# Normalisation and first projections in one stage: two weight chunks projected group by group of tokens

## The chip, the cores and the metric

One core of a Trainium2 chip runs the whole layer in one launch. The time is the device time of one execution in microseconds (us), three executions of the kernel before, and their median. One execution more was recorded by the profiler; all rows below are from it. TensorE is PE in the rows (PEld its weight loads), VectorE is DVE, ScalarE is ACT, GpSimd is POOL, SyncE is SP. SP and ACT each issue transfers (SPq, ACTq).

## What is computed

A layer of a streaming encoder: 2048 tokens of width 1024, float32. What matters here is its beginning:

```
c_act = silu(c)
mod = c_act @ ada_w[l] + ada_b[l]
sh1, sc1, g1, sh2, sc2, g2 = jnp.split(mod, 6, axis=-1)
h = modulate(rmsnorm(x, norm1_g[l]), sh1, sc1)      # h * (1 + sc1) + sh1
z = h @ w_in[l]
u_a, q, k, v, u_c = jnp.split(z, splits, axis=-1)
```

q and k are then RMS-normalised per half head and rotated (`apply_rope`). Behind this come three token mixers, their gates and merge, and a mixture of 32 experts; nothing of that is touched.

## The kernel before

The kernel is written as stages, one behind the other. Each engine has its own hand-written list of instructions, and semaphores order them between the engines; at the end of a stage all engines meet at a barrier (`Stage.end`, L136, L137). Float32 products are made of three passes: an operand is split in a high part (rounded to float32r, on ScalarE) and a low part (the rest, a subtraction on VectorE), and TensorE adds high by high, high by low and low by high.

**`stage_front`** (L162 and on) makes the columns and the normalised h.

- Shift and scale need the first 2048 columns of `ada_w`: eight pieces of 128 rows (1 MB each) are loaded in a ring of three (L197). VectorE multiplies each by its value of silu(c) and adds it up (L285, L288). TensorE sums over the partitions with 16 products by a column of ones (L269), and VectorE adds bias and `norm1_g` (L315, L316). `c`, the bias and `norm1_g` are loaded on ScalarE's queue, number by number (L215 to L217).
- x comes as 16 tiles of 128 tokens (L200), in a ring of eight. ScalarE squares and sums a tile and takes the root (L226, L228), VectorE the reciprocal (L292), and the tile is scaled, three of four on GpSimd (L251), the fourth on VectorE (L295).
- Then 32 pieces, four groups (`tb`) of 512 tokens by eight `k` of 128 channels: TensorE turns a piece (four 128 x 128 transposes, L264), ScalarE writes the high part of h with scale and shift (L234), VectorE makes the full value (`raised`, L302) and the low part (L309).

**`stage_project`** (L1489 and on) multiplies h by `w_in`: 16 chunks of 128 output columns by four groups, 64 units of 24 products (L1657 to L1659). In `chunks` (L1498) eight are z chunks (v, pooling and state-space inputs), stored as they are, and eight q or k chunks. The order is six z, four q/k, one z, four q/k, one z. A chunk's weights are loaded (L1539) into one buffer and split (L1670, L1737) into one of two pairs. A z unit is copied by ScalarE (L1723) and stored (L1599). A q or k unit is squared (L1679) and averaged by TensorE (L1644), rooted (L1694); VectorE takes the reciprocal (L1767), multiplies (L1770) and rotates (L1779, L1780, L1782); ScalarE and GpSimd split it (L1701, L1619), and two stores go out (L1558, L1559).

Two more jobs run beside the z chunks. VectorE makes the rotation's angles, 2048 wide (L1793 and on); ScalarE their sine and cosine. And the other four rows of `mod` are made of 32 pieces of `ada_w` (L1545, L1746, L1749), in numbers per unit that `pieces_by` gives. When eight pieces are in, TensorE sums them to a row (L1635) ahead of the unit that `ROW_AT` names (12, 16, 20, 23), VectorE adds the bias (L1756), and SP stores the row (L1552). The row buffers lie where the first q unit's squares go, so that one waits for the stores. At n = 30 SP issues a copy of h's second half to HBM (L1592, L1593).

In what follows a unit's number is its place in this order; unit 24 is the first q unit before.

```
units = [(c, tb) for c in range(NC) for tb in range(TB)]
def pieces_by(n):
    return max(0, min(4 * KD, int((n - 6) * 2.1)))
```

## Time and profile before

| | |
|---|---|
| median of three executions | 3270.24 us (3263.36 to 3271.16) |
| the profiled execution | 3264.71 us |
| its span in the profile | 3262.9 us |
| mean granted TensorE clock | 0.944 of full |
| PE, DVE, ACT, POOL busy | 2854.5, 1980.3, 1472.7, 383.4 us |

The span is cut into stages by the instructions at their ends: the normalisation ends at 113.0 us, the first product of the projection starts at 121.9 us, the attention stage at 556.0 us. Busy time is a sum over instructions; an idle stretch is named with what ended it. The granted clock (PEclk) is the mean over a stretch, where 1.00 is 2.4 GHz and 0.50 is 1.2 GHz.

### The profile page before, as it was taken

To read this page: it belongs to the slowest core of one execution; us is meant where nothing else is said; L and a number is where in the kernel's file an instruction comes from. 1 tells how busy PE (TensorE), PEld (TensorE's weight loads), DVE (VectorE), ACT (ScalarE), POOL (GpSimd) and SP (SyncE) were. 2 spreads that over 40 slices of the span, in tenths; PEclk is the share of its full clock that TensorE was granted. 3 is DMA by queue.
4 is the path that set the end of the run, shared out by engine and by line. 5 is a ranking of instruction groups with operands and counts; after the bars stand their busy time and mean duration, and the time that the engine had idled before them with its cause. 6 is when DMAs were issued, how large, how long until landed. Compare 5 with 4: busy or idle time off the path is not lost. (4 is left out here: it accounts for less than half of the span.)

```text
span 3262.9 us, 41708 instructions
## 1 busy us (share of the span) xinstructions
PE 2854.5 (87%) x13494; PEld 2215.7 (68%) x13495; DVE 1980.3 (61%) x3048; ACT 1472.7 (45%) x2363; POOL 383.4 (12%) x297
## 2 busy tenths in 40 slices
PE   2699898999999997799996897995899999999994
PEld 2576676676777766577774675884677777777772
DVE  5546986454545464533362665225788888888883
ACT  3313554554545452322232333122466666666662
POOL 3101211000000001110010000110122222222211
PEclk9799999999999998898897998997899999999997
DMA  5273434222222215411115997443797997876864
GB/s 215 60 239 118 154 104 124 80 88 81 77 89 65 85 54 199 126 49 39 39 55 193 317 284 271 162 168 129 271 315 252 356 356 257 272 229 206 278 197 135
DMA packets 289052, 553.56 MB, mean 170 GB/s; under 512 B 30745, under 2 KB 97561, under 8 KB 284834
## 3 DMA queue, kind: packets, MB, share of 16 engines
q1 hardware_dynamic: 266866, 500.43, 44.5%
q0 software_dynamic: 14112, 51.39, 6.6%
q8 instruction: 71, 1.16, 0.1%
q10 hardware_dynamic: 7952, 0.16, 0.1%
q14 instruction: 51, 0.42, 0.0%
HBM read 417.16 MB, written 143.15 MB: 172 GB/s over the span
## 5 line engine op out<-in xcount | busy, mean ns | idle before, releaser
L2484 DVE TENSOR_TENSOR moe_w_lo<-moe_W,moe_w_hi 128x1024 fp32r<-128x1024 f32 x392 | 470.8, 1221 | 83.3 <-ACT moe_w_hi L2420 81.2
L2420 ACT CAST moe_w_hi<-moe_W 128x1024 fp32r (+1 forms) x392 | 410.3, 1052 | 147.0 <-PE moe_h1b L2351 75.2
L1658 PE MATMUL project_bank<-h_lo,w_hi 128*128 128x512 f32 x512 | 204.7, 400 | 0.0
L682 DVE TENSOR_SCALAR_CACHE_REDUCE att_S<-att_bank 128x512 f32<-128x512 f32 x192 | 125.0, 689 | 121.5 <-PE att_bank L470 121.5
L503 PE MATMUL att_bank<-h_hi,w_hi 128*128 128x512 f32 x384 | 171.6, 447 | 12.3 <-PEq L137 9.0
L2376 PE MATMUL moe_yb<-moe_W,moe_hT 128*128 x384 | 172.6, 592 | 0.0
L2349 PE MATMUL moe_h1b<-moe_w_hi,moe_xT_hi 128*128 128x512 f32 x384 | 156.9, 409 | 3.8 <-DVE moe_xT_lo L2495 3.8
L588 ACT ACTIVATE att_S<-att_S,att_nm 128x128 f32<-128x128 f32 (+15 forms) x128 | 154.1, 1206 | 0.0
L504 PE MATMUL att_bank<-h_lo,w_hi 128*128 128x512 f32 x384 | 153.5, 400 | 0.0
L505 PE MATMUL att_bank<-h_hi,w_lo 128*128 128x512 f32 x384 | 152.9, 398 | 0.0
L2350 PE MATMUL moe_h1b<-moe_w_lo,moe_xT_hi 128*128 128x512 f32 x384 | 152.6, 397 | 0.0
L2351 PE MATMUL moe_h1b<-moe_w_hi,moe_xT_lo 128*128 128x512 f32 x384 | 152.4, 397 | 0.0
L2349 PE MATMUL moe_h3b<-moe_w_hi,moe_xT_hi 128*128 128x512 f32 x384 | 151.9, 396 | 0.0
L2350 PE MATMUL moe_h3b<-moe_w_lo,moe_xT_hi 128*128 128x512 f32 x384 | 151.9, 396 | 0.0
L2351 PE MATMUL moe_h3b<-moe_w_hi,moe_xT_lo 128*128 128x512 f32 x384 | 151.7, 395 | 0.0
L1928 PE MATMUL out_bank<-out_y_hi,out_w_hi 128*128 128x512 f32 x256 | 104.9, 410 | 52.3 <-DMA out_y_lo<-y_lo 31.8
L491 PEld LDWEIGHTS att_bank<-att_val,att_aT 128*128 128x128 f32 x1088 | 137.4, 191 | 17.5 <-ACT att_aT L596 5.0
L491 PE MATMUL att_bank<-att_val,att_aT 128*128 128x128 f32 x1088 | 146.3, 279 | 1.6 <-ACT att_aT L596 1.1
L470 PE MATMUL att_bank<-shared 64*128 64x512 f32 (+2 forms) x960 | 139.2, 396 | 1.3 <-DMA shared<-qk_lo 1.3
L2489 DVE TENSOR_TENSOR moe_w_lo<-moe_W,moe_w_hi 128x1024 fp32r<-128x1024 f32 x96 | 117.3, 1222 | 31.2 <-ACT moe_w_hi L2427 31.2
L679 DVE CUSTOM_DVE_ANT_0 att_S<-att_bank,consts 128x128 f32<-128x128 f32 (+3 forms) x128 | 57.7, 488 | 123.3 <-PE att_bank L470 123.2
L862 ACT ACTIVATE gate_out<-ssm_gate_bank,gate_gbt 128x512 f32<-128x512 f32 x42 | 28.8, 686 | 215.4 <-PE ssm_gate_bank L877 212.9
(461 smaller groups left out, 6958.6 us busy)
## 6 DMA issues: line engine op xcount, KB each, us to landing
moe_W<-in_moe_w SPq DMA_DIRECT2D x96, 2048.0 KB, 10.9
w_raw<-in_gate_w SPq DMA_DIRECT2D x48, 512.0 KB, 3.7
out_sg<-gateT SPq DMA_DIRECT2D x32, 768.0 KB, 8.1
gateT<-att_gates SPq DMA_DIRECT2D x48, 256.0 KB, 2.4
gateT<-gate_out SPq DMA_DIRECT2D x48, 256.0 KB, 2.3
front_w<-in_ada_w SPq DMA_DIRECT2D x8, 1024.0 KB, 7.8
front_x<-in_x SPq DMA_DIRECT2D x16, 512.0 KB, 6.4
w_raw<-in_w_in SPq DMA_DIRECT2D x16, 512.0 KB, 4.4
```

Source lines behind the costliest of these rows:

```text
L491: mm = pe.matmul(bank[6][:, 0:P], aT[:, n % 2, j, :], val[:, 4 * c + j, :], start=4 * c + j == 0, stop=4 * c + j == i)
L503: pe.matmul(bank[7][:], w_hi[b][:, k, :], h_hi[:, k, at], start=k == 0, stop=False)
L504: pe.matmul(bank[7][:], w_hi[b][:, k, :], h_lo[:, k, at], start=False, stop=False)
L505: mm = pe.matmul(bank[7][:], w_lo[b][:, k, :], h_hi[:, k, at], start=False, stop=k == KD - 1)
L588: nc.scalar.activation(S[:, at, m, :n], S[:, at, m, :n], ACT.Exp, bias=nm[:, at, m:m + 1], accum_out=den[:, at, m:m + 1]).then_inc(q["expe ...
L1658: pe.matmul(bank[n % 4][:], w_hi[b][:, k, :], low[:, k, at], start=False, stop=False)
L2349: pe.matmul(to[:], xT_hi[:, k, :], w_hi[:, at, part], start=k == 0, stop=False)
L2350: pe.matmul(to[:], xT_hi[:, k, :], w_lo[:, at, part], start=False, stop=False)
L2351: mm = pe.matmul(to[:], xT_lo[:, k, :], w_hi[:, at, part], start=False, stop=k == KD - 1)
L2376: mm = pe.matmul(yb[nh][:], hT[:, k - KS, :], raw_2(at_raw, k, nh * 512, 512), start=False, stop=k == KF - 1)
L2420: nc.scalar.copy(w_hi[:, slot(p, first), :], raw(at, p)).then_inc(q["w13_high"], 1)
L2484: nc.vector.tensor_tensor(w_lo[:, own, :], raw(at, p), w_hi[:, own, :].bitcast(F32), ALU.subtract).then_inc(q["w1_low" if p < 4 else "w3_l ...
```

## The change

`stage_front` goes; its work is in `stage_project`.

- SP loads c first. Then four `ada_w` pieces and four x tiles in turn, the bias and `norm1_g` (number by number) and the constants, three more pieces, chunk 0, and piece 8 when the first is used. The eight pieces have rooms of their own (`early0` and `early1`, which lie where the second halves of h are written later); the sum is made in the eighth.
- x, a ring of eight tiles, lies in `spare`, which later holds angles and rows. Tiles 0 to 7 are squared before the columns are ready, the others a group ahead. VectorE scales the first four between its seventh and eighth add.
- Turns use banks 4 to 7, so that a turn waits for the piece four earlier.
- From group 1 on each turn is followed by six products: two `k` of a unit of the group before, chunks 0 and 1. So units 0 to 5 are made there; a unit of chunk 0 waits for the pieces of h two at a time. Units 6 and 7 (group 3) and the other chunks follow as before.
- There are seven z chunks ahead of the eight q/k chunks and one behind them. `ROW_AT` is 16, 20, 24, 27 and `pieces_by` begins at 12. The angles move from unit 0 to unit 8. The copy of h's second half stays at n = 30.

TensorE's list, from its start. Before:

```order
L269 MATMUL front_bank<-consts,front_acc 128x1 x16
L264 MATMUL front_bank<-consts,front_x 128x128 x128
L193 UNCONDITIONAL_BRANCH
L1624 UNCONDITIONAL_BRANCH
L1657 MATMUL project_bank<-h_hi,w_hi 128x512
L1658 MATMUL project_bank<-h_lo,w_hi 128x512
```

Now:

```order
L1581 MATMUL project_bank<-consts,early 128x1 x16
L1559 MATMUL project_bank<-consts,project_spare 128x128 x36
L1572 MATMUL project_bank<-h_hi,w_hi 128x512
L1573 MATMUL project_bank<-h_lo,w_hi 128x512
L1574 MATMUL project_bank<-h_hi,w_lo 128x512
L1572 MATMUL project_bank<-h_hi,w_hi 128x512
L1573 MATMUL project_bank<-h_lo,w_hi 128x512
L1574 MATMUL project_bank<-h_hi,w_lo 128x512
L1559 MATMUL project_bank<-consts,project_spare 128x128 x4
```

All 128 transposes stood ahead of the first product; now eight turns (32 transposes) and the first of group 1 stand alone, and each of the other 23 behind six products.

SP's list of transfers, from its start. Before:

```order
L197 DMA front_w<-in_ada_w 128x2048 x3
L203 DMA consts<-const_pack 128x1365
L200 DMA front_x<-in_x 128x1024
L197 DMA front_w<-in_ada_w 128x2048
L200 DMA front_x<-in_x 128x1024
```

Now:

```order
L1435 DMA ccol<-in_c 128x8x1
L1401 DMA early<-in_ada_w 128x2048
L1404 DMA project_spare<-in_x 128x1024
...
L1439 DMA project_bcol<-in_ada_b 128x16x1
L1440 DMA project_n<-in_norm_g 128x8x1
L1441 DMA consts<-const_pack 128x1365
L1401 DMA early<-in_ada_w 128x2048 x3
L1408 DMA w_raw<-in_w_in 128x8x128
L1401 DMA early<-in_ada_w 128x2048
L1404 DMA project_spare<-in_x 128x1024 x4
```

The three transfers of single numbers have moved from ScalarE's queue to SP's, one to its head and two behind eight large ones.

SP's list at the first q and k stores (`late_hi`, `late_lo` are the copy of h's second half). Before:

```order
L1552 DMA rows<-project_spare 1x1024
L1558 DMA qk_hi<-project_o_hi 128x512
L1559 DMA qk_lo<-project_o_lo 128x512
...
L1592 DMA late_hi<-shared 128x8192
L1593 DMA late_lo<-h_lo 128x8192
L1558 DMA qk_hi<-project_o_hi 128x512
```

Now:

```order
L1421 DMA rows<-project_spare 1x1024
L1494 DMA late_hi<-shared 128x8192
L1495 DMA late_lo<-h_lo 128x8192
L1427 DMA qk_hi<-project_o_hi 128x512
L1428 DMA qk_lo<-project_o_lo 128x512
```

The copy stood behind the stores of four units and now stands ahead of all of them.

The diff, cut to its core:

```diff
-def stage_front(nc, g, h_hi, h_lo):
...
-    NZ = 6
+def stage_project(nc, g, rooms, h_hi, h_lo, wt):
...
+    NZ, NF = 7, 8
...
-    chunks = z[:NZ] + qk[:4] + z[NZ:NZ + 1] + qk[4:] + z[NZ + 1:]
+    chunks = z[:NZ] + qk + z[NZ:]
     NC = len(chunks)
-    units = [(c, tb) for c in range(NC) for tb in range(TB)]
+    units = [(c, tb) for tb in range(TB) for c in range(2)] + [(c, tb) for c in range(2, NC) for tb in range(TB)]
...
-    ROW_AT = (12, 16, 20, 23)
+    ROW_AT = (16, 20, 24, 27)
+    XR, AR, W = 8, 7, 2 * D
+    early = [rooms[i // 4][:, i % 4 * W:(i % 4 + 1) * W] for i in range(AR + 1)]
+    sums = early[AR]
...
-        return max(0, min(4 * KD, int((n - 6) * 2.1)))
+        return max(0, min(4 * KD, int((n - 11) * 2.3)))
...
+        return 7 + c if c < 2 else TB * (c + 1)
...
+        x = spare[:].rearrange("p (r n) -> p r n", r=XR)
...
+                sp.dma_start(g["ccol"][:], g["c"].rearrange("a (k p) -> p (a k)", p=P), allow_slow_non_contiguous=True).then_inc(f["c_ready"], 16)
+                for k in range(4):
+                    load_early(k)
+                    load_x(k)
+                sp.dma_start(bcol[:], g["ada_b"][:, 0:W].rearrange("a (k p) -> p (a k)", p=P), allow_slow_non_contiguous=True).then_inc(f["consts"], 16)
+                sp.dma_start(n1[:], g["norm1_g"].rearrange("a (k p) -> p (a k)", p=P), allow_slow_non_contiguous=True).then_inc(f["consts"], 16)
+                sp.dma_start(g["consts"][:], g["const_pack"]).then_inc(f["consts"], 16)
+                for k in range(4, AR):
+                    load_early(k)
                 load_w(0)
-                sp.dma_start(pos, g["positions"].broadcast_to([P, T])).then_inc(q["small"], 16)
+                sp.wait_ge(f["added"], 1)
+                load_early(AR)
+                for i in range(4, XR):
+                    load_x(i)
+                sp.wait_ge(q["w_split"], 1)
+                load_w(1)
...
+                sp.wait_ge(q["w_split"], 2)
+                load_w(2)
+                for tb in range(2, TB):
+                    sp.wait_ge(f["turned"], KD * (tb - 1))
+                    for i in range(4 * tb, 4 * tb + 4):
+                        load_x(i)
+                    if tb > 2:
+                        store_z(2 * tb - 5)
+                    store_z(2 * tb - 4)
+                store_z(2 * TB - 5)
+                sp.wait_ge(f["turned"], KD * (TB - 1))
+                sp.dma_start(pos, g["positions"].broadcast_to([P, T])).then_inc(q["small"], 16)
+                sp.wait_ge(f["squared"], NT)
                 load_bias(0)
-                sp.wait_ge(q["w_split"], 1)
-                load_w(1)
-                for n in range(NU + 2):
-                    if n < NU and units[n][1] == 0:
+                for n in range(4, NU + 2):
+                    if n == 7:
+                        sp.wait_ge(q["w_split"], 3)
+                        load_w(3)
...
+                for i in range(NT):
+                    if not on_dve(i):
+                        pool.wait_ge(f["reduced"], i + 1)
+                        nc.gpsimd.tensor_scalar(x[:, i % XR, :], x[:, i % XR, :], ss[:, i:i + 1], None, ALU.mult).then_inc(f["scaled_pool"], 1)
...
+                def turn(n):
+                    tb, k = n // KD, n % KD
+                    if k == 0:
+                        pe.wait_ge(f["scaled_pool"], 3 * tb + 3)
+                        pe.wait_ge(f["scaled_dve"], tb + 1)
+                    if n >= 4:
+                        pe.wait_ge(f["h_high"], n - 3)
+                        pe.wait_ge(f["raised"], n - 3)
+                    for j in range(4):
+                        mm = pe.transpose(bank[4 + n % 4][:, j * P:(j + 1) * P], x[:, (4 * tb + j) % XR, k * P:(k + 1) * P], const(g, "ident"))
+                    mm.then_inc(f["turned"], 1)
+
+                def products(n, k0, k1):
+                    c, tb = units[n]
+                    if k0 == 0:
+                        if tb == 0:
+                            pe.wait_ge(q["w_split"], c + 1)
+                        free_bank(n - 4)
+                    if n < NF and c == 0:
+                        pe.wait_ge(f["h_split"], KD * tb + k1)
+                    b, high, low = c % 2, h_hi[tb // 2], h_lo[tb // 2]
+                    for k in range(k0, k1):
+                        pe.matmul(bank[n % 4][:], w_hi[b][:, k, :], high[:, k, at512(tb)], start=k == 0, stop=False)
+                        pe.matmul(bank[n % 4][:], w_hi[b][:, k, :], low[:, k, at512(tb)], start=False, stop=False)
+                        mm = pe.matmul(bank[n % 4][:], w_lo[b][:, k, :], high[:, k, at512(tb)], start=False, stop=k == KD - 1)
+                    if k1 == KD:
+                        mm.then_inc(q["summed"], 1)
...
+                pe.wait_ge(f["consts"], 48)
+                pe.wait_ge(f["added"], KD)
+                for k in range(2 * KD):
+                    mm = pe.matmul(bank[0][:, k:k + 1], sums[:, k * P:(k + 1) * P], const(g, "ones")[:, 0:1], start=True, stop=True)
+                mm.then_inc(f["col_summed"], 1)
+                for n in range(KD):
+                    turn(n)
+                pe.wait_ge(f["col_ready"], 1)
+                for n in range(KD, NT8):
+                    turn(n)
+                    tb, k = n // KD - 1, n % KD
+                    products(2 * tb + k // 4, k % 4 * 2, k % 4 * 2 + 2)
+                for n in range(2 * TB - 2, NU + 2):
...
-                        c, tb = units[n]
-                        if tb == 0:
-                            pe.wait_ge(q["w_split"], c + 1)
-                        free_bank(n - 4)
-                        at = slice(tb % 2 * 512, tb % 2 * 512 + 512)
-                        b, high, low = c % 2, h_hi[tb // 2], h_lo[tb // 2]
-                        for k in range(KD):
-                            pe.matmul(bank[n % 4][:], w_hi[b][:, k, :], high[:, k, at], start=k == 0, stop=False)
-                            pe.matmul(bank[n % 4][:], w_hi[b][:, k, :], low[:, k, at], start=False, stop=False)
-                            mm = pe.matmul(bank[n % 4][:], w_lo[b][:, k, :], high[:, k, at], start=False, stop=k == KD - 1)
-                        mm.then_inc(q["summed"], 1)
+                        products(n, 0, KD)
...
+                def high_x(n):
+                    tb, k = n // KD, n % KD
+                    act.wait_ge(f["turned"], n + 1)
+                    nc.scalar.activation(h_hi[tb // 2][:, k, at512(tb)], bank[4 + n % 4][:], ACT.Identity, scale=col[:, KD + k:KD + k + 1],
+                                         bias=col[:, k:k + 1]).then_inc(f["h_high"], 1)
...
+                        act.wait_ge(q["summed"], chunk_end(c - 2))
...
+                for i in range(4):
+                    square_x(i)
+                split(0)
+                for i in range(4, 8):
+                    square_x(i)
+                split(1)
+                act.wait_ge(f["col_ready"], 1)
+                for n in range(NT8):
+                    tb, k = n // KD, n % KD
+                    high_x(n)
+                    if 1 <= tb < TB - 1 and k < 4:
+                        square_x(4 * (tb + 1) + k)
+                    if tb >= 2 and k == 1:
+                        place_z(2 * tb - 3)
+                    if tb >= 1 and k == 5:
+                        place_z(2 * tb - 2)
...
+                place_z(2 * TB - 3)
+                for n in range(2 * TB - 2, NU + 2):
...
+                    if n == 11:
...
+                for k in range(KD):
+                    add(k)
+                    if k == 6:
+                        for i in range(4):
+                            scale(i)
                 split(0)
-                for n in range(NU + 2):
+                dve.wait_ge(f["consts"], 48)
+                dve.wait_ge(f["col_summed"], 1)
+                link(nc.vector.tensor_tensor(col[:], bank[0][:, 0:2 * KD], bcol[:], ALU.add))
+                nc.vector.scalar_tensor_tensor(col[:, KD:], col[:, KD:], 1.0, n1[:], ALU.add, ALU.mult).then_inc(f["col_ready"], 1)
+                dve.wait_ge(f["col_ready"], 1)
+                split(1)
+                for n in range(NT8):
+                    tb, k = n // KD, n % KD
+                    raise_x(n)
+                    if n >= 1:
+                        low_x(n - 1)
+                    if tb < TB - 1 and 1 <= k <= 4:
+                        scale(4 * (tb + 1) + k - 1)
+                low_x(NT8 - 1)
...
+        with nc.sbuf_tensor("early0", [P, KD * D], F32) as early0:
+            pass
...
+            with nc.sbuf_tensor("early1", [P, KD * D], F32) as early1:
+                pass
...
-                stage_front(nc, g, h_hi, [h_lo, h_lo1])
...
-                stage_project(nc, g, h_hi, [h_lo, h_lo1], wt)
+                stage_project(nc, g, [early0, early1], h_hi, [h_lo, h_lo1], wt)
```

## Rows read from the trace of the kernel before

**Rows 1.** Busy time by stage; columns: stretch, length, busy (count) by engine, PEclk, DMA share, GB/s.

```profile
48.10:113.00 64.90, 22.04 (x128) 21.18 (x128) 50.97 (x79) 38.19 (x68) 26.70 (x10) 0.71 0.18 65
121.90:275.00 153.10, 147.03 (x590) 111.03 (x591) 72.10 (x59) 24.17 (x32) 0.41 (x2) 0.96 0.54 175
427.60:556.00 128.40, 115.26 (x459) 85.39 (x457) 113.90 (x81) 67.67 (x113) 27.23 (x16) 0.98 0.30 91
```

**Rows 2.** Timeline of the start: start us, us, engine, line, operation, idle before.

```profile
1.86 12.79 ACTq L217 DMA_DIRECT2D front_n<-in_norm_g  x1
...
38.14 2.35 DVE L288 SCALAR_TENSOR_TENSOR front_acc<-front_w,ccol,front_acc 128x2048 f32<-128x2048 f32 x1 [1.41 <-DMA front_w<-in_ada_w]
...
40.64 6.96 PE L269 MATMUL front_bank<-consts,front_acc 128*128 128x1 f32 x32 [40.64 <-DVE front_acc L288]
40.67 8.53 POOL L251 TENSOR_SCALAR front_x<-front_x,front_ss 128x1024 f32<-128x1024 f32 x3 [39.85 <-DVE front_ss L292]
...
47.91 0.17 DVE L316 SCALAR_TENSOR_TENSOR front_col<-front_col,front_n 128x8 f32<-128x8 f32 x1
```

**Rows 3.** Busy time in two stretches of the start, columns as in rows 1.

```profile
16.00:18.00 2.00, 0.00 (x0) 0.00 (x0) 1.68 (x4) 1.98 (x4) 0.00 (x0) 1.00 0.03 0
32.00:36.00 4.00, 0.00 (x0) 0.00 (x0) 2.58 (x2) 1.32 (x3) 0.00 (x0) 1.00 1.02 420
```

**Rows 4.** Timeline of the normalisation: TensorE's turns of group 0, VectorE in group 1, its end.

```profile
49.26 5.04 PE L264 MATMUL front_bank<-consts,front_x 128*128 128x128 f32 x32 [1.67 <-POOL front_x L251]
...
67.65 0.81 DVE L302 TENSOR_SCALAR front_raised<-front_bank,front_col 128x512 f32<-128x512 f32 x1 [2.04 <-ACT h_hi L234]
...
71.92 0.99 DVE L309 TENSOR_TENSOR h_lo<-front_raised,h_hi 128x512 fp32r<-128x512 f32 x1
...
81.22 0.75 DVE L295 TENSOR_SCALAR front_x<-front_x,front_ss 128x1024 f32<-128x1024 f32 x1
...
111.72 1.28 DVE L309 TENSOR_TENSOR h_lo<-front_raised,shared 128x512 fp32r<-128x512 f32 x2
```

**Rows 5.** Timeline of TensorE in the projection.

```profile
121.91 0.79 PE L1657 MATMUL project_bank<-h_hi,w_hi 128*128 128x512 f32 x1 [17.46 <-DVE w_lo L1737]
...
158.08 0.40 PE L1657 MATMUL project_bank<-shared,w_hi 128*128 128x512 f32 x1
...
214.91 0.40 PE L1657 MATMUL project_bank<-shared,w_hi 128*128 128x512 f32 x1
...
216.08 0.40 PE L1659 MATMUL project_bank<-shared,w_lo 128*128 128x512 f32 x1
...
218.21 0.50 PE L1657 MATMUL project_bank<-h_hi,w_hi 128*128 128x512 f32 x1
...
265.90 3.57 PE L1635 MATMUL project_bank<-project_spare,consts 128*1 128x512 f32 x4 [6.07 <-DVE project_spare L1749]
...
275.60 0.39 PE L1657 MATMUL project_bank<-h_hi,w_hi 128*128 128x512 f32 x1
```

**Rows 6.** Timeline: pieces 6 and 7 of `ada_w`, issued and added.

```profile
181.75 0.43 SPq L1545 DMA_DIRECT2D project_o_hi<-in_ada_w  x1
...
189.69 1.28 DVE L1749 SCALAR_TENSOR_TENSOR project_spare<-project_o_lo,ccol,project_spare 128x1024 f32<-128x1024 f32 x1
```

**Rows 7.** Timeline of VectorE in the q and k chunks; last the copy's issue (KB, us to landing).

```profile
285.39 0.75 DVE L1779 SCALAR_TENSOR_TENSOR project_spare<-project_bank,project_gcol,project_spare 128x512 f32<-128x512 f32 x1 [6.79 <-ACT project_spare L1687]
...
346.05 1.38 DVE L1737 TENSOR_TENSOR w_lo<-w_raw,w_hi 128x1024 fp32r<-128x1024 f32 x1 [6.24 <-ACT w_hi L1670]
...
410.02 0.69 DVE L1770 TENSOR_TENSOR project_o<-project_spare 128x512 f32<-128x512 f32 x1
...
431.58 0.75 DVE L1779 SCALAR_TENSOR_TENSOR project_spare<-project_bank,project_gcol,project_spare 128x512 f32<-128x512 f32 x1
...
534.73 0.74 DVE L1779 SCALAR_TENSOR_TENSOR project_spare<-project_bank,project_gcol,project_spare 128x512 f32<-128x512 f32 x1
...
late_lo<-h_lo SPq DMA_DIRECT2D x1, 4096.0 KB, 23.0
```

More of the change, by code:

```diff
@@ L1529, in stage_project @@
         q = {n: s.sem(n) for n in names}
+        front_names = ("c_ready consts exped col_summed col_ready squared rooted reduced scaled_pool scaled_dve turned h_high raised h_split added").split()
+        f = {n: s.sem(f"x_{n}") for n in front_names}
+        early_ready = [s.sem(f"early_ready{i}") for i in range(AR)]
+        x_ready = [s.sem(f"x_ready{i}") for i in range(XR)]
         z_stored = [s.sem("z_stored0"), s.sem("z_stored1")]
@@ L1596, in _ @@
                     if n < NU and is_z[n]:
-                        i, (c, tb) = order[n], units[n]
-                        sp.wait_ge(q["copied"], i + 1)
-                        sp.dma_start(g["zT"][chunks[c][2], :, tb * 512:(tb + 1) * 512], oz[:, i % 2, :]).then_inc(z_stored[i % 2], 16)
+                        store_z(n)
                 for b in range(2):
@@ L1706, in _ @@
                 act.dma_start(g["gate_bias"][:], g["gate_b"].rearrange("a (k p) -> p (a k)", p=P), allow_slow_non_contiguous=True).then_inc(q["later"], 16)
-                split(0)
-                for n in range(NU + 2):
+                place_z(2 * TB - 3)
+                for n in range(2 * TB - 2, NU + 2):
                     if n >= 2 and not is_z[n - 2]:
                         high(n - 2)
-                    if n == 5:
+                    if n == 11:
                         act.wait_ge(q["biased"], 2)
@@ L1715, in _ @@
                         nc.scalar.activation(cos, tmp, ACT.Sin, scale=-1.0, bias=half_pi[:]).then_inc(q["sined"], 1)
-                    if n < NU and units[n][1] == 0:
+                    if n == 7:
+                        split(2)
+                    if NF <= n < NU and units[n][1] == 0:
                         split(units[n][0] + 1)
                     if n < NU and is_z[n]:
-                        i = order[n]
-                        act.wait_ge(q["summed"], n + 1)
-                        if i >= 2:
-                            act.wait_ge(z_stored[i % 2], 16 * (i // 2))
-                        nc.scalar.copy(oz[:, i % 2, :], bank[n % 4][:]).then_inc(q["copied"], 1)
+                        place_z(n)
                     if n < NU and not is_z[n]:
@@ L1783, in rope @@
                     dve.wait_ge(q["roped"], m + 1)
-                split(0)
-                for n in range(NU + 2):
+                dve.wait_ge(f["exped"], 1)
+                link(nc.vector.tensor_scalar(cexp[:], cexp[:], 1.0, None, ALU.add))
+                link(nc.vector.reciprocal(cexp[:], cexp[:]))
+                link(nc.vector.tensor_tensor(ccol[:], ccol[:], cexp[:], ALU.mult))
+                for k in range(KD):
[3 more added lines that the diff above has]
+                            scale(i)
+                split(0)
+                dve.wait_ge(f["consts"], 48)
[5 more added lines that the diff above has]
+                for n in range(NT8):
+                    tb, k = n // KD, n % KD
+                    raise_x(n)
[4 more added lines that the diff above has]
+                low_x(NT8 - 1)
+                for n in range(2 * TB - 2, NU + 2):
                     if n - 1 in ROW_AT:
                         finish_row(ROW_AT.index(n - 1))
-                    if n < NU and units[n][1] == 0:
+                    if n == 7:
+                        split(2)
+                    if NF <= n < NU and units[n][1] == 0:
                         split(units[n][0] + 1)
-                    if n == 0:
+                    if n == 8:
                         dve.wait_ge(q["small"], 16 * 13)
```

229 lines of the change are left out of this document (70 added, 159 removed).

## Prediction

> **What bounds the kernel now.** I read the busy shares of the stages first. The normalisation, 48.1 to 113 us, is nobody's: TensorE is busy 22.0 of 64.9 us, VectorE 51.0, ScalarE 38.2. The projection behind it is TensorE's, 147.0 of 153.1 us. In the q and k part VectorE and TensorE are close, 113.9 and 115.3 of 128.4 us, but there TensorE's 115.3 hold 16 units and a z chunk of 22.5, so 5.8 us a unit [rows 1], and VectorE needs 7.1 a unit (below). Then the timeline: between the last instruction of the normalisation, at 111.72 + 1.28 = 113.0 us [rows 4], and the first product at 121.91 us [rows 5] lie a barrier, a weight load and its split. So the stretch to 121.9 us is a chain of several engines, the next is TensorE's work, the last VectorE's. A change that projects during the normalisation gains TensorE's work there, as far as VectorE doesn't then end last.
>
> I follow one time through: C, when the shift and scale columns are ready. It is 47.91 + 0.17 = 48.1 us before [rows 2].
>
> **The start.** Before, the sums begin behind an issue on ScalarE's queue that took 12.79 us, to 14.65, and end at 38.14 + 2.35 = 40.5 us [rows 2]. The transfer engines stand still meanwhile: 0 GB/s at 16 to 18 us against 420 GB/s later [rows 3]. Now seven pieces have rooms and c comes first. Ahead of the end of the eighth piece lie 8 x 1.05 MB of ada_w, 4 x 0.52 MB of x, 0.70 MB of constants and a weight chunk of 0.52 MB: 11.7 MB, 27.9 us at 420 GB/s, from about 1.5 us on: 29.4. What the three transfers of single numbers (4096 in all) cost on SP's queue no row shows. Nothing, if they are prepared while the big ones drain; 12.8 us, if they go like the issue that stood. I take 5.5, below the middle, because two of the three follow eight big transfers: 34.9. With 1.1 to arrive, the last add starts at 36.0. It takes 2.35 us, and about 1.0 more because GpSimd now scales x beside it: a subtraction beside such a scaling took 0.99 us, two alone 1.28 [rows 4]. So 39.4; then the column sums as before, 6.96 us [rows 2], with 0.6 around them: **C = 47.0**. The split of chunk 0 hides under the column sums, and so does GpSimd's scaling of three tiles (8.53 us, begun only at 40.67 before [rows 2]).
>
> The Trainium skill, page "DMA: Bandwidth & Descriptors", section "Queues, rings and completion order", says that a transfer engine takes the descriptors of a ring in order. By that rule the small ones hold up what is behind them, and C moves towards rival 2.
>
> **Group 0.** Behind C VectorE splits chunk 1 (1.2 us) and then raises and subtracts, 0.81 + 0.68 to 0.99 us a piece [rows 4], with a reciprocal of the next group in each of pieces 1 to 4. The first falls at C + 3.8; GpSimd needs 3 x 2.84 us for its tiles: C + 12.4 = 59.4 us. Then the transposes of group 1 and the first products may begin. x tiles 4 to 7 are squared before C, and the second weight chunk arrives at about C.
>
> **Groups 1 to 3 with products.** A step of TensorE is one turn, 5.04 / 8 = 0.63 us [rows 4], and six products at (216.08 - 214.91) / 5 = 0.234 us [rows 5], 1.40: 2.03 us, 24 steps 48.8. VectorE needs 14.3 us for a group with the next one's reciprocals (67.65 to 81.22 + 0.75 [rows 4]), less than TensorE's 16.2; ScalarE had 38.2 us for all four groups [rows 1], under 10 each, and gets 1.2 of copies. So TensorE paces it: 108.2. It stands some 4 us before 59.4, and behind a gap its clock was at the lower of its two levels: the first product took 0.79 us after 17.46 us of waiting, 0.40 later [rows 5]. I add 2 us, and 1 until the last piece is subtracted: unit 6 starts at **111.2 us**, against 158.08 [rows 5]. Of these 46.9, 33.7 are six units of 5.62 us, 8.9 the stretch 113.0 to 121.9, 1.1 is C; the rest is the slow clock and the gaps of the groups.
>
> **The rest of the z chunks.** Units 6 to 27, 22 x 24 x 0.234 = 123.6 us, and four row sums, 218.21 - 216.08 less a product, 1.90 us each [rows 5]: 242.4. Ahead of the first row there is now one unit of slack instead of two: its pieces 6 and 7 are issued one unit before it. Before, this pair took from 181.75 to 189.69 + 1.28 = 191.0 us [rows 6], 9.2 against the 5.6 of a unit; with the queue's later start I get a stall of 5, and 1.5 for the clock. The last row stalled before, 6.07 us [rows 5]; piece 31 is now issued beside the two ahead of it, so I expect 3.4, with 0.5 for the clock. With these 10.4 the first q unit starts at **252.8**, against 275.60 [rows 5].
>
> **The q and k chunks.** Here VectorE's chain decides: 7.1 us a unit (431.58 to 534.73: 14 units and three splits of 1.2 us [rows 7]). The first rotation comes 285.39 - 275.60 = 9.8 us behind the unit's start, behind the store of row 3, which is ordered as before: 262.6. From first to last rotation it took 249.3 us (285.39 to 534.73 [rows 7]). Two parts of this go. The z chunk in the middle: from the end of the 16th unit (410.02 + 0.69) to the second rotation behind it (431.58) were 20.9, and a unit takes 7.1: 13.8. And the copy of h's second half to HBM (2 x 4.2 MB, landed 23.0 us after its issue) stood in front of q/k stores; VectorE lost 6.24 us to it, at 346.05 [rows 7]. Now it is issued ahead of the first of these stores and ends about when that one is due. Some of it returns, since VectorE's next addition again meets GpSimd; I count 5.3. What the moved z chunk covered, TensorE's catching up, isn't missed: 5.8 us a unit stay under 7.1. So 249.3 - 13.8 - 5.3 = 230.2: last rotation at 492.8. The last z chunk and the end are ordered as before: 21.3 us to attention's start (534.73 to 556.0), and 1 for more semaphores to clear: **515.1 instead of 556.0, 40.9 less**. What follows is untouched.
>
> **Sum.** The profiled execution took 3264.7 us (span 3262.9); 3264.7 - 40.9 = 3223.8. It lay 5.5 below the median, 3270.2, so I forecast **3229 us**. A difference of 0.3% (10 us) is about what a measurement of this kernel can tell from none.
>
> **The rivals.**
> 1. *The chain, not TensorE, paces groups 1 to 3.* With four banks a turn waits for the piece four earlier, and late x tiles hold ScalarE. At 2.5 us a step, 24 x 0.5 = 12: 3241. For it: the squares are bunched in four steps of eight. Against: the banks give a lead of 8 us. Chance 0.12.
> 2. *Small transfers hold the ring.* At 12.8 instead of 5.5, C becomes 54.3: 3236. For it: the issue of 12.79 us. Against: the big ones ahead give them time. Chance 0.15.
> 3. *The waits stay.* The copy still stops a q/k store (5.3), and the rows wait 2 longer: 3236. For it: both transfers were waited for before. Chance 0.12.
> 4. *Nothing in the way.* The small transfers cost nothing (5.5) and row 0 arrives in time (6.5): 3217. Chance 0.12.
> 5. *No overlap in effect.* If products wait for pieces as they come, the normalisation grows by what it takes in, 33.7 us, and 7 remain: 3263, no change that shows. Against: VectorE has 2 us a group to spare. Chance 0.03.
> 6. *Slower.* If turns, products and waits mix so that TensorE stays at its lower level from unit 6 on, a unit takes twice 5.62 us. The gain is used up after 7 such units; over 22 of them 124 us are lost: 3353. Against: the projection ran at 0.96 of the full clock, and the normalisation, a third of it busy, still at 0.71 [rows 1]. Chance 0.02.
>
> The forecast as worked out keeps 0.44. The range takes in rivals 1 to 4 and the bounds of the sum: 3216 to 3245. Its lower end is rival 4 with 1 us, its upper rival 1 with half of rival 3. Outside lie 5, 6 and combinations, together under 0.15. Faster by over 0.3% is nearly all but 5 and 6: 0.94; within 0.3%: 0.04; slower: 0.02.
>
> **What would show it.** In the profile after: the eighth add near 36 us and the column near 47; TensorE without gaps from near 59; a group of eight steps in 16 to 17 us; unit 6 near 111; a wait of some 5 us before the first row sum, 3 to 4 before the last; VectorE without a pause from 263 to 500 us and no wait of 6 us for a q/k store; attention's first product at 515. The forecast is wrong if C lies over 54, if a group takes over 19 us, if the clock stays low beyond 66 us, or if attention starts at 515 and the whole is not 40 us shorter.

## The result, and the profile after

The changed kernel took **3228.5 us** (median of 4 runs, 3225.6 to 3230.5) against 3270.3 of the kernel before beside it: ratio 0.9876, 95% interval 0.9859 to 0.9893, 41.8 us less. Forecast were 3229, with 3216 to 3245 as the range. The profiled execution took 3229.6 us (span 3227.3). It lies 1.0 above its median and that of before 5.5 below, so between the two traces there are only 35.2 us.

VectorE's timeline of the start of the changed kernel, and SyncE's queue (columns as in [rows 2]):

```profile
7.17 1.29 DVE L1717 TENSOR_SCALAR early<-early,ccol 128x2048 f32<-128x2048 f32 x1 [3.14 <-DMA early<-in_ada_w]
...
26.67 4.84 DVE L1720 SCALAR_TENSOR_TENSOR early<-early,ccol 128x2048 f32<-128x2048 f32 x2 [5.82 <-DMA early<-in_ada_w]
...
35.97 2.35 DVE L1720 SCALAR_TENSOR_TENSOR early<-early,ccol 128x2048 f32<-128x2048 f32 x1
...
45.74 0.17 DVE L1801 SCALAR_TENSOR_TENSOR project_col<-project_col,project_n 128x8 f32<-128x8 f32 x1
```

```profile
6.48 13.09 SPq L1440 DMA_DIRECT2D project_n<-in_norm_g  x1
19.61 0.58 SPq L1441 DMA_DIRECT2D consts<-const_pack  x1
```

The first addition starts at 7 us, not behind an issue of 12.79 us [rows 2]. That issue hasn't gone, it moved: norm1_g now holds SyncE's queue for 13.09 us, the constants and the last pieces of ada_w wait behind it, and the fifth addition starts after a gap of 5.82 us. The constants are issued at 19.61 us and the last four pieces of ada_w from 20.24 us on. The columns come at 45.74 + 0.17 = 45.9 us instead of 48.1.

TensorE's timeline of the changed kernel, where [rows 4, 5] stand for the kernel before:

```profile
58.89 1.09 PE L1559 MATMUL project_bank<-consts,project_spare 128*128 128x128 f32 x4 [5.88 <-POOL project_spare L1515]
59.63 0.78 PE L1572 MATMUL project_bank<-h_hi,w_hi 128*128 128x512 f32 x1
...
105.93 0.40 PE L1574 MATMUL project_bank<-shared,w_lo 128*128 128x512 f32 x1
108.58 0.71 PE L1572 MATMUL project_bank<-shared,w_hi 128*128 128x512 f32 x1 [2.26 <-ACT project_oz L1629]
...
172.09 3.57 PE L1539 MATMUL project_bank<-project_spare,consts 128*1 128x512 f32 x4 [5.51 <-DVE project_spare L1752]
...
253.77 0.40 PE L1572 MATMUL project_bank<-h_hi,w_hi 128*128 128x512 f32 x1
...
516.46 0.77 PE L336 MATMUL att_bank<-h_hi,w_hi 128*128 128x512 f32 x1 [10.83 <-PEq L137]
```

Unit 0 starts at 59.63 instead of 121.91 and unit 6 at 108.58 instead of 158.08. The first q unit starts at 253.77 instead of 275.60; there the kernel before had done 24 z units and this one 28. Attention starts at 516.46 instead of 556.04. What TensorE waited for before unit 6 was VectorE's last piece, which ended at 108.4 by the next row; the row names ScalarE's copy, but that ended just as late and the bank it frees isn't the one unit 6 takes. VectorE's last two subtractions:

```profile
107.15 1.28 DVE L1740 TENSOR_TENSOR h_lo<-project_o,shared 128x512 fp32r<-128x512 f32 x2
```

The stages of the changed kernel in three stretches, normalisation with six units, the rest of z, the end of q and k (columns as in [rows 1]):

```profile
45.90:108.50 62.60, 52.85 (x271) 43.58 (x269) 53.39 (x81) 37.67 (x62) 26.92 (x11) 0.92 0.32 115
108.50:253.77 145.27, 137.33 (x545) 102.34 (x546) 72.18 (x59) 22.97 (x30) 0.00 (x0) 0.95 0.54 178
380.00:516.40 136.40, 116.43 (x456) 84.30 (x454) 120.02 (x86) 69.75 (x117) 28.75 (x17) 0.97 0.32 97
```

The normalisation, which no engine bounded before (TensorE busy 22.0 of 64.9 us [rows 1]), now holds 52.9 us of TensorE in 62.6, and VectorE's 53.4 beside it. The q and k rotations (VectorE's line by itself; first and last start stand behind the durations):

```profile
L1782 DVE SCALAR_TENSOR_TENSOR project_spare<-project_bank,project_gcol,project_spare x32: 743/744/750, 263.6 to 493.3; 128x512 f32<-128x512 f32 x32
```

493.3 - 263.6 = 229.7 us, where it was 249.3. Of the two long waits of [rows 7] the one inside this stretch (6.24 us at 346.05) is gone. The one before the first rotation stays, 6.87 us where it was 6.79:

```profile
263.62 0.75 DVE L1782 SCALAR_TENSOR_TENSOR project_spare<-project_bank,project_gcol,project_spare 128x512 f32<-128x512 f32 x1 [6.87 <-ACT project_spare L1646]
```

So the 39.6 us at attention's start are made up like this: 49.5 at unit 6; less 27.7 from there to the first q unit, since that stretch now holds four units more (22.5 us) and took 145.2 us instead of 117.5; plus 19.6 in the rotations; less 1.9 from the last rotation to attention (23.2 us instead of 21.3).

### The profile page after: what moved, and what is told of

The parts are those of the page before. It is cut to its first block and busy times, and to the rows that moved or that the text cites. A ratio compares the mean times of both kernels' runs of the same rounds, so it can differ in the third digit from the quotient of the medians.

```text
span 3227.3 us, 41692 instructions
## 1 busy us (share of the span) xinstructions
PE 2858.8 (89%) x13494; PEld 2213.1 (69%) x13495; DVE 1984.2 (61%) x3048; ACT 1472.7 (46%) x2363; POOL 390.5 (12%) x296
```

## The experiments

All are edits of the changed kernel. The kernel before ran beside each, and kernels that did not run side by side are compared by their ratios to it, since these medians move by a few us. For the changed kernel it is 0.9876, and 0.9885 in a second measurement (below).

**1. The same stage, nothing laid over.** TensorE does all its turns, then the six units; ScalarE's copies and the z stores move behind.

```
 for n in range(KD, NT8):
     turn(n)
-    products(2 * tb + k // 4, k % 4 * 2, k % 4 * 2 + 2)
-for n in range(2 * TB - 2, NU + 2):
+for n in range(NU + 2):
```

> The merged stage stays, but TensorE does all 32 turns first and the first six units behind them. My theory (the gain is TensorE's work laid under the pieces of groups 1 to 3): the last piece is subtracted near 108 to 111 us as now, since VectorE paces it, and unit 6 starts 6 x 5.62 = 33.7 us later than in the changed kernel, at 142 to 146 instead of 108.6. Time 33 to 37 us above the changed kernel: 3262 to 3266, ratio 0.998 to 0.999. Rival (the barrier, the weight load and the split that the merged stage saves are most of it): at most 15 us above the changed kernel, unit 6 before 125.

Measured: 3252.7 us, ratio 0.9946 (0.9929 to 0.9962), 0.7% or 23 us above the changed kernel. In its trace:

```profile
95.22 0.81 DVE L1727 TENSOR_SCALAR project_o<-project_bank,project_col 128x512 f32<-128x512 f32 x1
...
102.02 1.28 DVE L1733 TENSOR_TENSOR h_lo<-project_o,shared 128x512 fp32r<-128x512 f32 x2
```

```profile
96.73 0.78 PE L1570 MATMUL project_bank<-h_hi,w_hi 128*128 128x512 f32 x1
...
539.34 0.77 PE L336 MATMUL att_bank<-h_hi,w_hi 128*128 128x512 f32 x1 [10.81 <-PEq L137]
```

Neither theory held: above the rival's 15, below my 33. Alone the pieces are done at 102.02 + 1.28 = 103.3 us, 5.1 earlier than with products between the turns, and TensorE, four turns ahead of them, starts unit 0 at 96.7, under the last four pieces. Unit 6 starts at 131.9 us instead of 108.6. So the six units (33.7 us) laid over save 539.34 - 516.46 = **22.9 us** at attention's start. The rest comes without any overlap: from columns to first product it was 121.9 - 48.1 = 73.8 us and is 96.73 - 45.9 = 50.8 here, 23.0 less. Of these 8.9 are the barrier, the weight load and its split (113.0 to 121.9), 6.6 the start under the last pieces (103.3 - 96.7), 7.5 the normalisation itself (64.9 to 57.4).

**2. The single numbers on ScalarE's queue.** The waits for them move too; the edit's core:

```
-sp.dma_start(bcol[:], ...).then_inc(f["consts"], 16)
-sp.dma_start(n1[:], ...).then_inc(f["consts"], 16)
 nc.scalar.activation(cexp[:], ..., ACT.Exp, scale=-1.0)
+act.dma_start(bcol[:], ...).then_inc(f["few"], 16)
+act.dma_start(n1[:], ...).then_inc(f["few"], 16)
```

> The 3072 single numbers (ada_b, norm1_g) go from SyncE's queue to ScalarE's, behind the exponential that needs c. My theory: on SyncE's queue their issue of 13.09 us held back the fifth ada_w piece; the transfer engines moved 331 and 182 GB/s at 16 to 19 and 20 to 23 us instead of 420, some 3.5 us of transfer. So the last addition starts at about 32.5 instead of 35.97, the columns are ready at 42.4 instead of 45.9, and the whole takes 3.5 us less: 3225. Rival (single numbers cost the transfer engines the same from any queue): no change, columns at 45.9, 3228.5. Second rival (ScalarE's squares come late and hold VectorE's reciprocals, which stand before the last addition): columns later than 46.

Measured: 3226.3 us, ratio 0.9876 (0.9859 to 0.9892): no difference. Timeline of this kernel, the two long issues and the last addition:

```profile
3.54 15.03 ACTq L1601 DMA_DIRECT2D project_n<-in_norm_g  x1
9.74 14.97 SPq L1401 DMA_DIRECT2D early<-in_ada_w  x1
...
34.52 2.35 DVE L1720 SCALAR_TENSOR_TENSOR early<-early,ccol 128x2048 f32<-128x2048 f32 x1 [0.69 <-DMA early<-in_ada_w]
...
44.33 0.17 DVE L1802 SCALAR_TENSOR_TENSOR project_col<-project_col,project_n 128x8 f32<-128x8 f32 x1
```

Busy time of two stretches, first this kernel, then the changed one (columns as in [rows 1]):

```profile
8.00:11.00 3.00, 0.00 (x0) 0.00 (x0) 0.46 (x2) 0.00 (x0) 0.00 (x0) 1.00 1.01 399
20.00:23.00 3.00, 0.00 (x0) 0.00 (x0) 1.07 (x1) 2.96 (x6) 0.00 (x0) 1.00 1.05 413
```

```profile
8.00:11.00 3.00, 0.00 (x0) 0.00 (x0) 0.50 (x2) 2.47 (x4) 0.00 (x0) 1.00 0.99 415
20.00:23.00 3.00, 0.00 (x0) 0.00 (x0) 0.85 (x1) 1.44 (x3) 0.00 (x0) 1.00 0.86 182
```

The hole at 20 us is gone, but the rate is lower elsewhere: 399 instead of 415 GB/s here, and 302 instead of 371 from 29 to 32 us. And SyncE's queue stands too, 14.97 us at the issue of the eighth 1 MB piece. The columns come 1.4 us earlier, not 3.5. That the rest is the transfer engines' own time for the single numbers fits these rates, but no run shows it apart.

**3. A z chunk among the q and k chunks.** `chunks = z[:NZ] + qk[:4] + z[NZ:] + qk[4:]` instead of `z[:NZ] + qk + z[NZ:]`.

> The last z chunk stands behind the first four q/k chunks instead of at the end. My theory (VectorE's chain bounds the q/k part, a z chunk there is added in full): from the first to the last rotation 229.7 + 13.8 = 243.5 us; at the end the z chunk's cover is missing, but what follows the last rotation is VectorE's and the store's own tail, so the stage ends 10 to 14 us later: 3238 to 3243. Rival (TensorE needs the z chunk to catch up or the chunk at the end costs as much as in the middle): total within 3 us of the changed kernel, 3226 to 3232.

Measured: 3238.4 us, ratio 0.9909 (0.9892 to 0.9926), 10 us more than the changed kernel. The rotations:

```profile
L1782 DVE SCALAR_TENSOR_TENSOR project_spare<-project_bank,project_gcol,project_spare x32: 743/744/752, 266.3 to 509.4; 128x512 f32<-128x512 f32 x32
```

243.1 us instead of 229.7, so the chunk adds 13.4; I had taken 13.8 from [rows 7]. Of it 5.4 us come back at the end, from the last rotation to attention's start (527.2 - 509.4 = 17.8 us, 23.2 in the changed kernel), while the first rotation stood 2.7 us later in this trace. The rival falls: TensorE doesn't need it to catch up.

**4. The first row sum a unit later.** `ROW_AT = (17, 20, 24, 27)` instead of `(16, 20, 24, 27)`.

> The first row sum stands a unit later (17 instead of 16), nothing else. My theory: the 5.51 us that TensorE stands before it go, and about 1 us of lower clock behind them: first q unit at 247.5 instead of 253.8, total 6 us less, 3222. Rival (the bound is the arrival of the pieces, so the wait turns up at the next or the last row): stalls of rows 1 to 3 grow from 2.4 to 5 us and more, and the total falls by less than 2 us.

Measured: 3219.5 us, ratio 0.9852 (0.9836 to 0.9869), 0.24% or 8 us below the changed kernel, where 6 were expected. TensorE at the first row, and the rotations:

```profile
170.46 1.88 PE L1539 MATMUL project_bank<-project_spare,consts 128*1 128x512 f32 x4 [0.75 <-DVE project_spare L1752]
```

```profile
L1782 DVE SCALAR_TENSOR_TENSOR project_spare<-project_bank,project_gcol,project_spare x32: 743/745/750, 254.6 to 484.2; 128x512 f32<-128x512 f32 x32
```

The first rotation is 9.0 us earlier. TensorE's waits before row sums fall from 7.9 to 3.5 us in all, and unit 6 stood 1.0 earlier (107.62). The rest is the clock. Its granted clock from 170 to 180 us was 0.66 of the full one in the changed kernel and 1.00 here, and the first row sum with the four products behind it took 5.12 us there and 2.84 here, so 2.3 us were lost; another 1.6 were lost behind unit 6's start, where this trace has the full clock. Those 1.6 and the 1.0 aren't the edit's: the changed kernel's second trace (experiment 9) has the full clock there too, and against it the first rotation is 8.0 us earlier.

```profile
170.00:180.00 10.00, 7.91 (x20) 0.66 0.58 208
```

```profile
170.00:180.00 10.00, 9.54 (x37) 1.00 0.67 223
```

(TensorE alone: stretch, length, busy, granted clock, DMA share, GB/s; the changed kernel, then this one.) Why the pieces were late in the changed kernel: the first is issued at 152.56 us, behind the sine (145.63) that waits for VectorE's angles (125 to 144), though the addition itself takes only 1.3 us a piece. That is read from one trace; no run moves the angles.

**5. The late copy behind four q/k stores again.** `if n == 34:` instead of `if n == 30:`.

> The copy of h's second half goes out four units later (n = 34 instead of 30), behind four q/k stores as before the change. My theory: its 2 x 4.2 MB stand in front of a q/k store again and VectorE waits some 6 us at one of GpSimd's subtractions; from first to last rotation 229.7 + 5.3 = 235 us, total 5 us more, 3234. Rival (the order alone doesn't matter, since the q/k part now has fewer transfers beside it): rotations 229.7 to 231, total within 1 us of the changed kernel.

Measured: 3233.7 us, ratio 0.9899 (0.9883 to 0.9916). VectorE waits 6.54 us again, as it did at 346.05 before [rows 7]:

```profile
322.30 1.37 DVE L1711 TENSOR_TENSOR w_lo<-w_raw,w_hi 128x1024 fp32r<-128x1024 f32 x1 [6.54 <-ACT w_hi L1622]
```

Its rotations run from 261.4 to 496.9 us, 235.5 instead of 229.7: 5.8 us, expected 5.3. The total is 5 to 8 us above the changed kernel's two measurements. So the order of the copy accounts for the wait of 6.24 us before the change.

**6. Tiles 4 to 7 scaled ahead of the columns.**

```
 split(0)
+for i in range(4, 8):
+    scale(i)
 dve.wait_ge(f["consts"], 48)
...
-    if tb < TB - 1 and 1 <= k <= 4:
+    if 1 <= tb < TB - 1 and 1 <= k <= 4:
```

> The reciprocals of x tiles 4 to 7 and VectorE's scaling of tile 7 move from behind the columns to the 6 us in which VectorE waits for the column sums. My theory: the first turn of group 1 waited 5.88 us for GpSimd, which got its tiles 4 to 6 only after pieces 1 to 4; now GpSimd has them at 44.9 us, behind tiles 0 to 2, and ends near 55: the turn starts at 55.7 instead of 58.9, VectorE has 2.2 us less to do behind the columns, unit 6 starts 3 us earlier (105.5) and the total is 3 us less, 3225.5. Rival (from the columns on the chain of pieces paces all, and GpSimd's tiles only hide behind it): unit 6 and the total unchanged within 1 us.

Measured: 3220.2 us, ratio 0.9857 (0.9840 to 0.9873), 6 to 9 us below the changed kernel. GpSimd, and TensorE's first turn of group 1 and unit 6:

```profile
34.06 19.56 POOL L1515 TENSOR_SCALAR project_spare<-project_spare,project_ss 128x1024 f32<-128x1024 f32 x6 [33.21 <-DVE project_ss L1724]
```

```profile
53.72 0.64 PE L1559 MATMUL project_bank<-consts,project_spare 128*128 128x128 f32 x4 [1.12 <-POOL project_spare L1515]
...
102.70 0.47 PE L1572 MATMUL project_bank<-shared,w_hi 128*128 128x512 f32 x1 [1.79 <-DVE h_lo L1740]
```

GpSimd goes through six tiles without a pause, the turn starts at 53.7 instead of 58.9, and unit 6 at 102.7 instead of 108.6: all of it arrives. So the chain from the columns to group 1 ran over GpSimd's tiles.

**7. Products in the wait before group 1.**

```
+for k in range(0, 6, 2):
+    products(0, k, k + 2)
 for n in range(KD, NT8):
     turn(n)
+    if n == KD:
+        products(0, 6, 8)
+    if tb == 0: products(1, k, k + 1)
+    else:       products(2 * tb + k // 4, ...)
```

> Eighteen of the 24 products of unit 0 stand ahead of the first turn of group 1, where TensorE waited 5.88 us; in group 1 a turn has three products behind it instead of six. My theory (TensorE paced group 1 at 2.03 us a step, VectorE 1.79): group 1 takes 14.3 instead of 16 us, groups 2 and 3 as they were, unit 6 at 107 instead of 108.6, total 1 to 2 us less. Rival (VectorE was behind already, it ended its last piece 2.3 us after TensorE was done): nothing, within 1 us, and TensorE only waits elsewhere.

Measured: 3228.7 us, ratio 0.9885 (0.9869 to 0.9902): no gain, and its unit 6 has to wait for pieces that end at 110.80 + 1.28 = 112.1 us instead of 108.4. TensorE waits where it didn't:

```profile
59.06 0.50 PE L1572 MATMUL project_bank<-h_hi,w_hi 128*128 128x512 f32 x1 [3.09 <-DVE h_lo L1747]
...
64.17 0.79 PE L1572 MATMUL project_bank<-h_hi,w_hi 128*128 128x512 f32 x1 [2.31 <-DVE h_lo L1747]
...
79.45 0.66 PE L1559 MATMUL project_bank<-consts,project_spare 128*128 128x128 f32 x4 [3.69 <-POOL project_spare L1515]
```

TensorE takes its list in order: products that wait for VectorE's pieces hold back the turns that VectorE would go on with, and then both wait. The filler has to be something that is ready.

**8. Experiments 2, 4, 6 and 7 together.**

> Single numbers on ScalarE's queue, row 0 a unit later, tiles 4 to 7 scaled early, and the wait filled, together. My theory, each by its own: 2.2 measured, 9.0 measured, 3 and 1.5 expected: 15 us less than the changed kernel, 3213 to 3215, ratio to the kernel before 0.983 to 0.984. Rival (they gain on the same slack): 3217 to 3220, no better than row 0 alone.

Measured: 3221.1 us, ratio 0.9852 (0.9835 to 0.9868): the rival's case. The traces point at the products of experiment 7: unit 6 starts at 109.16 us, and at 100.93 in experiment 12, which lacks only these products. The intervals of the two totals overlap a little.

**9. The changed kernel again.**

> The changed kernel once more, on the chip of the three that follow. Both theories: 3226 to 3231, ratio to the kernel before 0.986 to 0.990. Its trace tells how much the clock's dips and the later stages move from one execution to the next: attention starts at 516.46 in the first, and 3 us of the difference to the kernel before are lost behind it.

Measured: 3230.0 us, ratio 0.9885 (0.9869 to 0.9900). Attention starts at 515.4 us in its trace. The first MoE product starts 1760.0 us after it (2275.4), where it was 1757.2 in the first trace (2273.7 - 516.46), 1753.9 in the kernel before (2309.9 - 556.04) and 1753.0 in experiment 10. So the stages behind attention's start took 7 us more or less in these four traces, with the same instructions; over all traces it is 1750.7 (experiment 12) to 1760.1 (experiment 1).

**10. Squares and reciprocals at the pace of before.** ScalarE: `k % 2 == 0: square_x(4 * (tb + 1) + k // 2)` instead of `k < 4: square_x(4 * (tb + 1) + k)`; VectorE: `k % 2 == 1: scale(4 * (tb + 1) + k // 2)` instead of `1 <= k <= 4`.

> Squares and reciprocals of the next group stand behind every second piece again, as before the change, not behind the first four. My theory: the last x tile of a group is then scaled behind piece 7; the first turn of group 1 starts 4.6 us later (before it stood 17.6 us behind the columns, now 13.0), and of groups 2 and 3 a little later too, since a group took 16.4 us before and TensorE now needs 15.7: unit 6 near 115, total 6 us more, 3234. Rival (only TensorE's load counts there): group 1 later by 4.6, made up for by shorter waits after it; total within 1.5 us.

Measured: 3229.8 us, ratio 0.9888 (0.9873 to 0.9903), the same as experiment 9 beside it. But its trace has both theories in it:

```profile
60.52 1.08 PE L1559 MATMUL project_bank<-consts,project_spare 128*128 128x128 f32 x4 [7.58 <-issue]
...
113.01 0.47 PE L1572 MATMUL project_bank<-shared,w_hi 128*128 128x512 f32 x1 [1.61 <-DVE h_lo L1740]
```

Group 1 starts 1.7 us later, not 4.6, TensorE waits before groups 2 and 3 too, and unit 6 starts 4.4 to 5.3 us later than in the two traces of the changed kernel. Attention starts 2 to 3 us later (518.4). The total doesn't show it; an effect of 3 us is below what these intervals tell. What the squares' pace is worth is 2 to 3 us by the traces and not settled by the times.

**11. Experiments 4 and 6 together.**

> Row 0 a unit later and x tiles 4 to 7 scaled before the columns. Alone they brought the first rotation from 263.6 to 254.6 and 258.1. My theory (they lie behind one another on TensorE's path): first rotation near 249.5, total 13 to 15 us below the changed kernel, 3214 to 3216. Rival (an earlier unit 6 makes TensorE wait longer for the pieces, whose start hangs on the sine and VectorE's 17 us of angles): first rotation at 253 or later, total no better than row 0 alone, 3219.

Measured: **3212.8 us**, ratio 0.9834 (0.9820 to 0.9847), 0.5% or 17 us below the changed kernel beside it. Rotations:

```profile
L1782 DVE SCALAR_TENSOR_TENSOR project_spare<-project_bank,project_gcol,project_spare x32: 742/744/751, 246.4 to 476.1; 128x512 f32<-128x512 f32 x32
```

The first is at 246.4, 3 us before my 249.5: from unit 6 (102.21) to it are 144.2 us, where it was 155.0 in the changed kernel. Two short waits before rows are left, 0.40 and 2.01 us, and the granted clock is full in each stretch from 108 to 264 us.

**12. The same with the single numbers on ScalarE's queue.**

> As the one before, and the single numbers on ScalarE's queue (columns 1.4 us earlier). My theory: another 1.4 to 2 us: 3212 to 3214, the best of all. Rival (as in the four together, which had the filled wait too and took 3221): it isn't the filled wait that spoiled that one, and this takes 3218 or more.

Measured: 3214.5 us, ratio 0.9833 (0.9820 to 0.9847): not to be told from experiment 11, as experiment 2 had it. In its trace unit 6 starts 1.3 us earlier (100.93), but TensorE waits 2.88 us before the last row and the clock falls behind it (0.88 from 226 to 240 us), so the first rotation comes at 247.3, 0.9 later. The 1.4 us reach unit 6 and no further. By the ratios it is 6 us under experiment 8.

## Why the prediction was right

The time and its sign came out, and so did most of the steps; that the total fits to 1 us is partly luck, since errors of 2.6 and 3.6 us, and later of 5.8 and 6.5, cancelled. Forecast and profile, in us:

| | forecast | after |
|---|---|---|
| last addition starts | 36.0 | 36.0 |
| columns (C) | 47.0 | 45.9 |
| first turn of group 1 | 59.4 | 58.9 |
| unit 6 | 111.2 | 108.6 |
| first q unit | 252.8 | 253.8 |
| first, last rotation | 262.6, 492.8 | 263.6, 493.3 |
| attention | 515.1 | 516.5 |
| own time | 3223.8 | 3229.6 |

- *The start.* The sum with 5.5 us for the single numbers put the last addition to 36.0, and it began at 35.97. Of the two bounds, 0 and 12.8, neither was right: the issue stood 13.09 us, but the transfer engines had four big pairs to drain meanwhile. The 5.5 was a choice between the bounds, so its fit is luck in part; and VectorE's own list ended at the same moment (the scaling of a tile, 34.40 + 1.55 = 35.95), a bound the sum didn't have. By experiment 2 the queue is worth 1.4 us of it; what the rest is stays open. The Trainium skill, page "DMA: Bandwidth & Descriptors", section "Queues, rings and completion order", has a transfer engine take a ring's descriptors in order. The gap of 5.82 us before the fifth addition doesn't show that: the fifth piece was issued only at 20.24 us, behind the issue of 13.09 us, which explains the gap by itself. And C didn't move towards rival 2's 54.3. The 1.0 us for an addition beside GpSimd didn't come: 2.35 us, as alone, which is nearly all of the 1.1 us that C was early. GpSimd paid instead, 10.64 us for three tiles and not 8.53.
- *Group 0.* C + 12.4 was C + 13.0 for the turn, and the reason given (GpSimd's tiles behind the reciprocals) is shown by experiment 6, which moved these and the fourth tile's scaling and got 5.2 us at the turn.
- *Groups 1 to 3.* 24 steps took 105.93 + 0.23 - 58.89 = 47.3 us, forecast 48.8 and 2 for the clock. The turn was sized too long, 0.63 us: a step at the full clock (100.66 to 102.50) takes 1.84 us, of which 1.40 are products, so a turn adds 0.44. TensorE paces it (busy 46.8 of the 47.3 us), VectorE is 2.3 us behind at the end (forecast 1). Rival 1 (2.5 us a step) fell. So unit 6 stood 2.6 us ahead of the forecast.

```profile
100.66 0.60 PE L1559 MATMUL project_bank<-consts,project_spare 128*128 128x128 f32 x4
...
102.50 0.60 PE L1559 MATMUL project_bank<-consts,project_spare 128*128 128x128 f32 x4
```

- *The z chunks.* From unit 6 to the first q unit 145.2 us, forecast 141.6. Row 0 stalled 5.51 (forecast 5), the last row 2.34 (3.4). The clock is the mis-sized term: 1.5 + 0.5 us were counted. Its granted shares were 0.86 (108 to 120), 0.66 (170 to 180) and 0.89 (240 to 256). Part of this low clock fell into TensorE's own waiting and cost nothing; from start to start of the same instructions at the full clock in other traces, 1.6 + 2.3 + 1.6 = 5.5 us were lost. This ate what unit 6 had won, 2.6 us early against 3.6 late: two errors that cancelled, and that is luck.
- *The q and k part.* 229.7 us, forecast 230.2. Both terms are shown alone: z chunk 13.4 (13.8) by experiment 3, late copy 5.8 (5.3) by experiment 5. Behind the last rotation it took 23.2 us, forecast 22.3. Rival 3 fell: no wait for a q/k store is left, and the rows wait 7.9 us in all, not 10.4.
- *Behind it.* 39.6 us won at attention's start, 40.9 forecast. The missing 4 us to the own time of 3229.6 lie in untouched stages, within the 7 us by which these move (experiment 9). The forecast of the median took over that the profiled execution before lay 5.5 us below it; the one after lay 1.0 above, so the 5.8 us by which the own time was missed went against 6.5 us from the executions' scatter. The two profiled executions differ by 35.2 us, the medians by 41.8.

Two things in the bookkeeping were wrong or left out. First, though no number of the sum hung on it, the prediction split the 46.9 us of unit 6 into 33.7 for the six units, 8.9 for the barrier and 1.1 for C, and by that gave 3263 us to rival 5, no overlap in effect. Experiment 1 is that case and took 3252.7. The overlap is worth 22.9 us, since products between the turns slow the pieces and, without them, TensorE's first units slide under the last pieces anyway. The whole change without its overlap is already worth 16 to 19 us (its 3252.7 against 3268.3 beside it, and 41.8 - 22.9), and the moved z chunk and copy are in that.

Second, the prediction counts the seventh z chunk's way out of the q and k part as a gain of 13.8 us and its four units ahead of it inside the 22 of the z chunks, and never sets one against the other. In the old place it costs 13.4 us (experiment 3), ahead of the q and k chunks four units of 5.62 = 22.5 us. So, by an estimate from these two, this part of the change by itself loses some 9 us. No run has six z chunks ahead again, and whether the pieces of ada_w would then be in time for the rows is open.

## What to carry to other kernels

Work laid over another stage is worth its own length less what it delays there, and less what would have slid under it anyway: count the gain against the merged stage without overlap, not against the kernel before. In an in-order engine, fill a wait only with work whose inputs are ready, or it moves the wait to its supplier. A chunk moved out of one stage's bound goes into another's: price both places. A stall of the engine that bounds can cost more than its length, because of the clock behind it: two cheap moves, a row sum a unit later and the scaling of four tiles into an idle stretch, brought 3213 us, 0.5% under the changed kernel.

## What the runs showed of the hardware

- An issue can stand long on either queue, and what it carries doesn't tell which. The 1024 numbers of norm1_g stood 12.79 us on ScalarE's queue [rows 2], 13.09 on SyncE's, 15.03 on ScalarE's beside running transfers; the 2048 of ada_b, just ahead of them, 0.71 us on SyncE's and 0.45 on ScalarE's. And with both gone from SyncE's queue a 1 MB piece stood there for 14.97 us (experiment 2). Why is open. Moving the single numbers off the queue of the big transfers brought 1.4 us at the columns.
- The same gap doesn't always cost the same clock. Before unit 6 TensorE waited 2.26 to 2.29 us in six traces with the same order up to there. In those of the changed kernel and of experiments 3 and 5 the first product behind it took 0.71 to 0.77 us and the next 0.63, and the granted clock was 0.86 from 108 to 120 us; in those of experiments 2, 4 and 9 it was 0.47 us and a clock of 1.00. So a wait's price has a part that changes from one execution to the next, here 0 or 1.6 us.
- GpSimd and VectorE slow one another unevenly: three scalings of GpSimd took 10.64 us beside a scaling, an addition and a split of VectorE, and 8.53 before, beside a scaling alone; VectorE's addition kept its 2.35.
